# Half-sized weight requests for the sixth and seventh expert, moved ahead of a small table's store, and a vector's load moved behind them

## The chip, the cores and the metric

One core of one Trainium2 chip runs the whole kernel. The metric is the device time of one execution in microseconds (us), from a median of three runs. The core has a matrix engine (TensorE, PE in the rows), a vector engine (DVE), a scalar engine (ACT), GpSimd (POOL), and SyncE (SP), which here only asks for transfers. Sixteen DMA engines carry the transfers that SP's queue (q1 in the profile) and POOL's queue (q0) ask for.

## What is computed

One decoder layer over 1024 prompt tokens and 64 sample tokens, 1024 wide: a mixer (S5 and RG-LRU), cross attention, a mixture of experts, and a final norm. The change lies in the mixture of experts:

```python
def _hier_moe(x, g, w_group, w_expert, w_gate, w_up, w_down):
    hf = _rmsnorm(x, g).reshape(bsz * s, D_MODEL)
    ...                                    # top 1 of 4 groups, then top 2 of its 8 experts
    act = jax.nn.silu(jnp.einsum("td,edf->tef", hf, w_gate)) * jnp.einsum("td,edf->tef", hf, w_up)
    out = jnp.einsum("tef,efd->td", act * combine[..., None].astype(act.dtype), w_down)
    return out.reshape(bsz, s, D_MODEL).astype(x.dtype)
```

There are 32 experts; each has a gate and an up matrix of 1024 x 256 floats (1 MB each) and a down matrix of 256 x 1024 floats (1 MB). The kernel's output is the norm of x + out, times the vector `g_final`.

## The kernel before

The engines' programs are written out by hand, each engine in its own function, with semaphores between them; nothing reorders them. In the last stage the tokens are sorted by expert into slots: each expert has 96 slots, and 24 rounds of 128 slots go through all 32 experts, four thirds of an expert per round (`expert_of`). Rounds 0 and 1 use experts 0, 1 and 2. A round j is, on TensorE: `rows_t` (L1292, the gathered rows of a later round turned), `prod_t` (L1311), `gate_up(j + 1)` (L1304, 64 matmuls over k = 0 to 7) and `down(j)` (L1318, 32 matmuls). `gate_up(1)` is cut in two, k = 0 to 3 and k = 4 to 7, with the turn of round 2's rows between.

Weights go through rings of buffers in the on-chip memory: five slots for gate and up together (`gu`, GUB = 5) and five for down (`dn`). Experts 0 to 4 are loaded before the rounds begin. Expert e + 5 takes the slot of expert e, so its load waits until the last round that uses e has been through `gate_up` (semaphore `gu_full`, one per round) or `down` (`d_full`). `last_round(e)` says which round that is: 1 for experts 0 and 1, then 2 for experts 2 and 3, and so on. All these loads are issued by SP, in program order, `load_gu` as two transfers of 1 MB (L487), `load_dn` as one (L490).

POOL gathers the rows of each round by an indirect transfer (`fetch`, L640) from a table in memory, `work_rows`, whose row is the token's 1024 values and a tail of four values (its routing weights). Rounds 0 to 3 are gathered before the tails are there, and get theirs by small gathers of their own (L650). The tails are then stored by SP (`weights_out(xrows[:, D:RW], "wt_st")`, two transfers, L439 and L440: 1088 rows of 16 bytes). SP waits for the gathers of rounds 0 to 3 before that store (L531), since it writes the table that they read. POOL's gather of round 4 waits for `wt_st` (L704), and round 4's rows are turned by TensorE between `down(1)` and `gate_up(3)`. On POOL the store of round 0's result (L645) and the gather of round 5 come next.

`gfin` is `g_final` copied to all 128 partitions (L533, 512 KB); it is first used by the vector engine when the first finished rows are scaled (L2708).

Around the change SP's program is: the down weights of expert 4; the wait for the gathers of rounds 0 to 3; the tails' store; `gfin`; then, for each round, the loads that its end lets go.

Of the kernel before, what the change touches and what calls it, by code (L numbers as in the profile page):

```python
# [7 lines left out]
D = 1024  # L8
P = 128
# [17 lines left out]
NG, NE, FF = 4, 32, 256  # L27
# [3 lines left out]
GUB, DNB, XGB = 5, 5, 5  # L31
# [27 lines left out]
ys5_ok w_sum wout_in q_full q_free q_sum wo_in0 wo_in1 x_res0 x_res1 x_res2 sq2_ok xn2_ok xn2_st0  # L59
xn2_st1 mx_ok pn_ok smx_ok spn_ok ck_in0 ck_in1 ck_in2 cv_in0 cv_in1 cv_in2 consts_ok route_ok gexp_ok  # L60
a_ok r48_ok ctl_ok idx_ok gu_in0 gu_in1 gu_in2 gu_in3 gu_in4 dn_in0 dn_in1 dn_in2 dn_in3 dn_in4
xg_in0 xg_in1 xg_in2 xg_in3 t_full t_free gu_full silu_ok prod_ok rk_full ix_full dve_x ht_full htm_ok
d_full ya_ok zt_ok y_st0 y_st1 x_go xw_in role_ok wt_ok wt_st yg_in0 yg_in1 yg_in2 yg_in3
o_st0 o_st1 o_st2 o_st3 z_ok ss_ok pw_arg pw_ok std2_ok o_ok own_ok xg_in4 y_st2
yg_in4 o_st4 gath_in"""
# [2 lines left out]
def hybrid_layer(nc, I, O, W):  # L68
# [5 lines left out]
    with ctx:  # L74
# [3 lines left out]
        sem = {n: ctx.enter_context(nc.semaphore(n)) for n in SEMS.split()}  # L78
# [238 lines left out]
        gu = [reg(a, 2, KD, FF) for a in (0, 4096, 8192, R_UT, R_UT + 4096)]  # L317
        dn = [reg(a, 2, D) for a in [R_E2 + 2048 * s for s in range(4)] + [R_R]]
        RW = D + WT
# [5 lines left out]
        gfin = reg(R_Y + D * YGB, D)  # L325
# [5 lines left out]
        xrows = nc.dram_tensor("work_rows", (TOK, RW), f32, kind="Internal").ap()  # L331
# [16 lines left out]
        def expert_of(j, t):  # L348

            return ((0, 0, 1, 1), (0, 1, 2, 2))[j][t] if j < 2 else (4 * j + t) // 3  # L350

        def last_round(e):

            return max(1, (3 * e + 2) // 4)
# [5 lines left out]
        def _(sp):  # L360
# [77 lines left out]
            def weights_out(table, done):  # L438
                sp.dma_start(table[0:SEQ, :].rearrange("(i p) c -> p i c", p=P), wt[:, 0:NT - 1, :]).then_inc(sem[done], 16)  # L439
                sp.dma_start(table[SEQ:TOK, :], wt[0:ROWS[NT - 1], NT - 1, :]).then_inc(sem[done], 16)  # L440
# [44 lines left out]
            def load_gu(e, slot, s):  # L485
                for h, w in enumerate(("w_gate", "w_up")):
                    sp.dma_start(gu[slot][:, h, :, :], weights(w, e, "p k")).then_inc(s, 16)  # L487

            def load_dn(e, slot, s):
                sp.dma_start(dn[slot][:, :, :], weights("w_down", e, "k p")).then_inc(s, 16)  # L490

# [35 lines left out]
            weights_out(wtab, "lam_in")  # L527
            sp.wait_ge(sem["xg_in1"], 16)
            load_dn(4, 4, sem["dn_in4"])
            for c in range(4):  # L530
                sp.wait_ge(sem[f"xg_in{c}"], 16)  # L531
            weights_out(xrows[:, D:RW], "wt_st")
            sp.dma_start(gfin[:, :], I["g_final"].to_broadcast([P, D])).then_inc(sem["glu_in"], 16)  # L533
            for j in range(NR + 1):
                for e in range(NE - GUB):
                    if last_round(e) == j:
                        sp.wait_ge(sem["gu_full"], j + 1)
                        load_gu(e + GUB, e % GUB, sem[f"gu_in{e % GUB}"])
                for e in range(NE - DNB):
                    if last_round(e) == j - 1:  # L540
                        sp.wait_ge(sem["d_full"], j)
                        load_dn(e + DNB, e % DNB, sem[f"dn_in{e % DNB}"])
# [226 lines left out]
        def _(pe):  # L769
# [99 lines left out]
            for j in range(7):  # L869
                last = nc.tensor.transpose(b[:, j * GP:j * GP + GP], q16[0:GP, 11 + j, :], ident[0:GP, 0:GP])  # L870
            last.then_inc(sem["tp_full"], 1)
            pe.wait_ge(sem["bnat_in"], 16 * 18)
            for ri in range(2):
                b = claim(TP, tp, "tp_free")
                for j in range(4):
                    last = nc.tensor.transpose(b[:, j * P:j * P + P], craw[:, ri, j, :], ident[:, :])
# [3 lines left out]
            for ri in range(2):  # L880
                last = nc.tensor.transpose(b[:, ri * P:ri * P + P], stin[ri], ident[:, :])
# [7 lines left out]
            for q in range(4):  # L889
                for ri in range(2):  # L890
                    for j in range(4):
                        gp = q * 4 + j
                        for l in range(2):
                            last = nc.tensor.matmul(bl[l][32 * j:32 * j + GC, q * P:q * P + P], bbar[64 * l:64 * l + 64, ri, gp, :],
                                                    hmat[64 * l:64 * l + 64, ri, gp, 0:L, :].rearrange("p t c -> p (t c)"), start=ri == 0, stop=ri == 1)
# [5 lines left out]
            for gp in range(GP):  # L901
                b = claim(TAY, ta, "ta_free")
                for ri in range(2):
                    for l in range(2):
                        last = nc.tensor.matmul(b[64 * l:64 * l + 64, ri * CS:ri * CS + CS], gmat[:, gp, ri, 64 * l:64 * l + 64],
                                                uch[:, 2 * gp + l, :], start=True, stop=True)
# [52 lines left out]
            for t0, t1 in TSPLIT:  # L959
                for m in range(CT):  # L960
                    b = claim(MA, ma, "ma_free")
                    for k in range(CT):
                        last = nc.tensor.matmul(b[:, 0:(t1 - t0) * CS], wglu[:, k, m * P:m * P + P], yd[:, k, t0 * CS:t1 * CS], start=k == 0, stop=k == CT - 1)  # L963
# [9 lines left out]
            for ri in range(2):  # L973
                last = nc.tensor.transpose(b[0:GP, (2 + ri) * P:(3 + ri) * P], finp[:, ri, :], ident[:, :])
# [322 lines left out]

            def gate_up(j, k0=0, k1=KD):
                for e in experts(j):
                    pe.wait_ge(sem[f"gu_in{e % GUB}"], (e // GUB + 1) * 32)  # L1300
                for k in range(k0, k1):
                    for t in range(4):
                        e, t0 = expert_of(j, t), QT * t
                        last = nc.tensor.matmul(bank[2 + j % 2][t0:t0 + QT, :].rearrange("p (h n) -> p h n", h=2), (xgt[j % 2] if j else xgt_first)[:, k, t0:t0 + QT],  # L1304
                                                gu[e % GUB][:, :, k, :], start=k == 0, stop=k == KD - 1)
                if k1 == KD:
                    last.then_inc(sem["gu_full"], 1)

# [128 lines left out]
            for j in range(1, NR):  # L1437
# [12 lines left out]
                if j == NR - 2:  # L1450
# [6 lines left out]
                    for nh in range(2):  # L1457
                        last = residual(j, nh, False)
# [12 lines left out]
            with pe.If(pe.value_load(ctl[0:1, XT:XT + 1], min_val=0, max_val=XT) > 0):  # L1471
                pe.wait_ge(sem["o_ok"], NR)
                for c in (NR - 2, NR - 1):
                    for nh in range(2):
                        last = down_half(c, nh)
# [1379 lines left out]
```

## Time and profile before

| | |
|---|---|
| times of three runs | 1103.89, 1108.48, 1109.3 us; median 1108.48 |
| profiled execution, its own time | 1104.57 us, span 1102.8 us |
| TensorE busy | 1064.1 us, 96% of the span |
| VectorE, ScalarE, GpSimd busy | 63%, 26%, 17% |
| DMA | 204.97 MB, mean 186 GB/s over the span; 412 to 415 GB/s in most of the slices from 860 to 1050 us |

The span is what lies between the first and the last instruction of the profiled execution; 1.8 us lie around it. "DMA share" in the rows is the mean busy share of the 16 DMA engines in a stretch (1.00 is all of them, a little above is rounding at the edges), and GB/s what they moved. A share near 1 with few GB/s means that the engines hold packets that move slowly. Times in rows are from the span's start. In a row of the chain "DMA arena<-in_w_up" with its microseconds is the time from the request of a load to its landing.

### The profile page before, as it was taken

What the parts mean: (1) busy time and instruction counts of PE and PEld (TensorE: products, weight loads), DVE (VectorE), ACT (ScalarE), POOL (GpSimd) and SP (SyncE); (2) the same over time, 40 slices, a digit from 0 to 9 for tenths busy, and PEclk for the clock granted to TensorE, in tenths of its full rate; (3) what the DMA queues carried; (4) which work ended last, traced back from release to release, by engine and by line L of the source; (5) the groups of instructions that cost most, each with busy time, mean ns of one, the idle gap of its engine ahead of it and who ended that gap; (6) DMA issues with size and microseconds to landing.
All of it is one profiled execution on the core that took longest, in us unless ns stands there. A gap on an engine that the chain in (4) does not pass through costs nothing.

```text
span 1102.8 us, 15605 instructions
## 1 busy us (share of the span) xinstructions
PE 1064.1 (96%) x6135; PEld 607.6 (55%) x6135; DVE 695.9 (63%) x1385; ACT 289.4 (26%) x588; POOL 186.2 (17%) x229
## 2 busy tenths in 40 slices
PE   6999999999999999999999999989999999998996
PEld 4666766787764445888766645545533333333331
DVE  5576699947858665743376676877754455555453
ACT  5200341567821111100033301111411222222223
POOL 4000200101000000000000000000123445554455
PEclk9999999999999999999999999999999999999999
DMA  9109450297546004100244450015889999999962
GB/s 297 56 1 213 46 43 1 92 276 257 216 170 182 1 1 155 74 1 1 85 183 154 155 226 39 20 58 208 299 283 412 413 413 413 414 415 412 413 256 82
DMA packets 75468, 204.97 MB, mean 186 GB/s; under 512 B 25592, under 2 KB 34448, under 8 KB 67056
## 3 DMA queue, kind: packets, MB, share of 16 engines
q1 hardware_dynamic: 54336, 168.82, 43.4%
q0 software_dynamic: 20928, 35.09, 9.6%
q8 instruction: 50, 0.82, 0.3%
q14 instruction: 26, 0.21, 0.1%
q10 hardware_dynamic: 128, 0.03, 0.0%
HBM read 195.23 MB, written 52.18 MB: 224 GB/s over the span
## 4 chain that ended last, share of the span: by engine, by line
PE 77%; DMA 10%; DVE 5%; ACT 2%; SPq 2%; issue 2%; ACTq 0%; POOL 0%; POOLq 0%; DVEq 0%
PE bank L832 16%; PE bank L1004 9%; PE bank L1069 9%; PE bank L1304 8%; DMA arena<-in_w_up 7%; PE bank L1199 6%; PE bank L1318 4%; PE bank L802 3%; PE bank L963 3%; PE bank L1101 3%; PE bank L1166 3%; DMA arena<-in_w_down 2%; DMA arena<-work_rows,slots_in 1%; SPq L487 1%; PE bank L1248 1%
## 5 line engine op out<-in xcount | busy, mean ns | idle before, releaser
L832 PE MATMUL bank<-arena 128*128 128x360 f32 (+1 forms) x576 | 177.7, 468 | 0.9 <-DVE arena L1881 0.9
L1304 PE MATMUL bank<-arena 128*32 128x512 f32 x1536 | 172.3, 599 | 5.9 <-DMA arena<-in_w_up 5.9
L832 PEld LDWEIGHTS bank<-arena 128*128 128x128 f32 x576 | 108.5, 190 | 64.7 <-issue 1.4
L1304 PEld LDWEIGHTS bank<-arena 128*32 128x32 f32 x1536 | 50.4, 110 | 107.5 <-issue 107.1
L2200 DVE TENSOR_TENSOR arena<-arena,bank 128x512 f32<-128x512 f32 (+3 forms) x56 | 68.4, 1221 | 64.9 <-PE bank L1069 37.4
L1004 PE MATMUL bank<-arena 128*128 128x272 f32 x448 | 103.0, 392 | 0.0
L1199 PE MATMUL bank<-arena 128*128 128x512 f32 x224 | 100.6, 598 | 2.2 <-DVE arena L2365 2.2
L1069 PE MATMUL bank<-arena 128*128 128x512 f32 x224 | 97.7, 593 | 0.0
L1004 PEld LDWEIGHTS bank<-arena 128*128 128x128 f32 x448 | 85.0, 190 | 17.4
L1318 PE MATMUL bank<-arena 128*32 128x512 f32 x768 | 87.5, 593 | 1.3 <-DMA arena<-in_w_down 0.8
L2696 DVE SCALAR_TENSOR_TENSOR arena<-arena 128x1024 f32<-128x1024 f32 x22 | 45.8, 2083 | 66.5 <-ACT arena L1763 66.5
L1523 ACT ACTIVATE arena<-bank 128x272 f32<-128x272 f32 (+5 forms) x94 | 41.8, 450 | 170.4 <-PE bank L832 122.1
L1069 PEld LDWEIGHTS bank<-arena 128*128 128x128 f32 x224 | 41.9, 190 | 50.6 <-issue 50.6
L1199 PEld LDWEIGHTS bank<-arena 128*128 128x128 f32 x224 | 41.0, 190 | 47.6 <-issue 47.5
L1673 ACT ACTIVATE arena<-arena 128x1024 f32<-128x1024 f32 (+1 forms) x18 | 19.0, 1057 | 170.4 <-DVE arena L2200 151.5
L802 PE MATMUL bank<-arena 128*128 128x256 f32 x256 | 57.7, 382 | 0.3 <-ACT arena L1523 0.2
L1318 PEld LDWEIGHTS bank<-arena 128*32 128x32 f32 x768 | 26.3, 110 | 56.4 <-issue 55.7
L802 PEld LDWEIGHTS bank<-arena 128*128 128x128 f32 x256 | 47.8, 190 | 10.5 <-issue 4.4
L640 POOL DMA_INDIRECT arena<-work_rows,slots_in x24 | 27.9, 1162 | 149.9 <-DVE slots_in L2577 117.8
L2705 DVE TENSOR_TENSOR arena<-arena 128x1024 f32<-128x1024 f32 x22 | 26.9, 1224 | 39.2 <-DMA arena<-work_firsts,ptmp 39.2
L2288 DVE TENSOR_TENSOR arena<-bank,arena 128x272 f32<-128x272 f32 x48 | 20.4, 440 | 47.5 <-PE bank L1004 47.4
L1881 DVE TENSOR_TENSOR arena<-bank,par 128x512 f32<-128x512 f32 (+1 forms) x58 | 35.8, 657 | 21.1 <-PE bank L788 19.9
(474 smaller groups left out, 1457.3 us busy)
## 6 DMA issues: line engine op xcount, KB each, us to landing
arena<-in_w_gate SPq DMA_DIRECT2D x32, 1024.0 KB, 18.9
arena<-in_w_up SPq DMA_DIRECT2D x32, 1024.0 KB, 25.1
arena<-in_w_down SPq DMA_DIRECT2D x32, 1024.0 KB, 26.4
arena<-in_ck SPq DMA_DIRECT2D x8, 1024.0 KB, 7.1
arena<-in_cv SPq DMA_DIRECT2D x8, 1024.0 KB, 5.4
arena<-in_w_in SPq DMA_DIRECT2D x3, 2048.0 KB, 13.7
work_firsts<-in_x SPq DMA_DIRECT2D x1, 4352.0 KB
arena<-in_x SPq DMA_DIRECT2D x8, 512.0 KB, 5.9
```

The lines of the kernel that those rows point to most:

```text
L802: last = nc.tensor.matmul(b[:, 0:KQ], mt_[:, k, m * P:m * P + P], wkv[q % 3][:, k, :], start=k == 0, stop=k == KD - 1)
L832: last = nc.tensor.matmul(b[:, 0:w], win[slot][:, k, m * P:m * P + P], ht[:, k, c0:c0 + w], start=k == 0, stop=k == KD - 1)
L963: last = nc.tensor.matmul(b[:, 0:(t1 - t0) * CS], wglu[:, k, m * P:m * P + P], yd[:, k, t0 * CS:t1 * CS], start=k == 0, stop=k == CT - 1)
L1004: last = nc.tensor.matmul(b[:, 0:QN], a_(k, m), b_(k)[:, QN * n:QN * n + QN], start=k == 0, stop=k == 3)
L1069: last = nc.tensor.matmul(b[:, :], a_(k), b_(k), start=k == 0, stop=k == 3)
L1199: last = nc.tensor.matmul(b[:, :], a_(k), b_(k), start=k == 0, stop=k == 3)
L1304: last = nc.tensor.matmul(bank[2 + j % 2][t0:t0 + QT, :].rearrange("p (h n) -> p h n", h=2), (xgt[j % 2] if j else xgt_first)[:, k, t0:t0 ...
L1318: last = nc.tensor.matmul(bank[DB[j] + nh][t0:t0 + QT, :], htr[j % 2][:, k, t0:t0 + QT], dn[e % DNB][:, k, nh * 512:nh * 512 + 512], start ...
L1523: nc.scalar.activation(out, bank[ring[n % len(ring)]][0:out.shape[0], 0:w] if isinstance(w, int) else w(bank[ring[n % len(ring)]]), func, ...
L1881: V.tensor_tensor(out_cols(hf), b[:, :].rearrange("p (k t) -> p k t", k=4)[:, :, 0:r], cols[:, 4 * hf:4 * hf + 4].unsqueeze(2).to_broadcas ...
L2200: V.tensor_tensor(out, out, bank[banks(n)][:, :].unsqueeze(1).to_broadcast([P, width, 512]), ADD).then_inc(sem["md_free"], 1)
L2696: V.scalar_tensor_tensor(split(y), by_column(xg[b]), m1[:, slot:slot + 1], split(y), MUL, ADD).then_inc(sem["zt_ok"], 1)
```

## The change

The gate and up weights of experts 5 and 6 (the sixth and seventh; they take the slots of experts 0 and 1, whose last round is round 1) are each loaded as two halves of k, so eight transfers of 512 KB instead of four of 1 MB. The halves for k = 0 to 3 wait for a new semaphore, `gu_half`, which TensorE raises at k = 3 of every `gate_up`; those for k = 4 to 7 wait for `gu_full` as before. The first halves stand ahead of the wait for the gathers and the tails' store, the second halves behind it; `gfin` comes after them. The counts that `gate_up` waits for follow (`gate_fills`). The sizes of all other loads, and the order of all others, stay.

```diff
+        def in_halves(e):
+            return e >= GUB and last_round(e - GUB) == 1
+        def gate_fills(e):
+            return sum(64 if in_halves(o) else 32 for o in range(e % GUB, e + 1, GUB))
...
+            def load_gu_half(e, slot, k0):
+                for h, w in enumerate(("w_gate", "w_up")):
+                    sp.dma_start(gu[slot][:, h, k0:k0 + 4, :], weights(w, e, "p k")[:, k0:k0 + 4, :]).then_inc(sem[f"gu_in{slot}"], 16)
...
-            for c in range(4):
-                sp.wait_ge(sem[f"xg_in{c}"], 16)
-            weights_out(xrows[:, D:RW], "wt_st")
-            sp.dma_start(gfin[:, :], I["g_final"].to_broadcast([P, D])).then_inc(sem["glu_in"], 16)
             for j in range(NR + 1):
+                for k0 in (0, 4):
+                    for e in range(NE - GUB):
+                        if last_round(e) == j and in_halves(e + GUB):
+                            sp.wait_ge(sem["gu_full" if k0 else "gu_half"], j + 1)
+                            load_gu_half(e + GUB, e % GUB, k0)
+                    if (j, k0) == (1, 0):
+                        for c in range(4):
+                            sp.wait_ge(sem[f"xg_in{c}"], 16)
+                        weights_out(xrows[:, D:RW], "wt_st")
                 for e in range(NE - GUB):
-                    if last_round(e) == j:
+                    if last_round(e) == j and not in_halves(e + GUB):
                         sp.wait_ge(sem["gu_full"], j + 1)
                         load_gu(e + GUB, e % GUB, sem[f"gu_in{e % GUB}"])
+                if j == 1:
+                    sp.dma_start(gfin[:, :], I["g_final"].to_broadcast([P, D])).then_inc(sem["glu_in"], 16)
...
                 for e in experts(j):
-                    pe.wait_ge(sem[f"gu_in{e % GUB}"], (e // GUB + 1) * 32)
+                    pe.wait_ge(sem[f"gu_in{e % GUB}"], gate_fills(e))
...
+                    if k == 3:
+                        last.then_inc(sem["gu_half"], 1)
```

SP's program before, from the down weights of expert 4 (first row) to the down weights that the end of round 1 lets go (last row). `arena` is the on-chip memory, `work_rows<-wt` the tails, and a bracket names the semaphores that a request waits for:

```order
L490 DMA arena<-in_w_down 128x2x1024 [waits xg_in1]
L439 DMA work_rows<-wt 128x8x4 [waits xg_in2,xg_in3,xg_in1,xg_in0]
L440 DMA work_rows<-wt 64x4
L533 DMA arena<-in_g_final 128x1024
L487 DMA arena<-in_w_gate 128x2048 [waits gu_full]
L487 DMA arena<-in_w_up 128x2048
...
L490 DMA arena<-in_w_down 128x2x1024 [waits d_full] x2
```

The same place now, first as far as the tails' store (line numbers are those of the changed kernel):

```order
L502 DMA arena<-in_w_down 128x2x1024 [waits xg_in1]
L499 DMA arena<-in_w_gate 128x1024 [waits gu_half]
L499 DMA arena<-in_w_up 128x1024
L499 DMA arena<-in_w_gate 128x1024 [waits gu_half]
L499 DMA arena<-in_w_up 128x1024
L447 DMA work_rows<-wt 128x8x4 [waits xg_in2,xg_in3,xg_in1,xg_in0]
L448 DMA work_rows<-wt 64x4
```

and on from there to the first loads that round 2 lets go:

```order
L499 DMA arena<-in_w_gate 128x1024 [waits gu_full]
L499 DMA arena<-in_w_up 128x1024
L499 DMA arena<-in_w_gate 128x1024 [waits gu_full]
L499 DMA arena<-in_w_up 128x1024
L557 DMA arena<-in_g_final 128x1024
L495 DMA arena<-in_w_gate 128x2048 [waits gu_full]
```

Four requests have come ahead of the tails, and the vector has gone from in front of experts 5 and 6 to behind them; it still stands ahead of round 2's loads.

POOL's program keeps its order. Its place that depends on the tails, as it stands now (L669 the small gathers, L659 a gather of rows, L664 the store of a round's result):

```order
L669 DMA arena<-work_wtab,slots_in 128x4 [waits xg_in3]
L659 DMA arena<-work_rows,slots_in 128x1028 [waits wt_st]
L664 DMA work_firsts<-arena,slots_in 1088x1024 [waits zt_ok,small_out,idx_ok]
L659 DMA arena<-work_rows,slots_in 128x1028 [waits zt_ok]
L664 DMA work_firsts<-arena,slots_in 1088x1024 [waits zt_ok]
```

Nothing moved there; the gather of round 4 still waits for the tails, and the store of round 0's result and the gather of round 5 still stand behind it.

## Rows read from the trace of the kernel before

**Rows 1.** Page: the span, busy times, and the DMA lines of forty slices.

```profile
span 1102.8 us, 15605 instructions
PE 1064.1 (96%) x6135; PEld 607.6 (55%) x6135; DVE 695.9 (63%) x1385; ACT 289.4 (26%) x588; POOL 186.2 (17%) x229
GB/s 297 56 1 213 46 43 1 92 276 257 216 170 182 1 1 155 74 1 1 85 183 154 155 226 39 20 58 208 299 283 412 413 413 413 414 415 412 413 256 82
```

**Rows 2.** Windows of the last stage: stretch, length, busy engines, clock, DMA share, GB/s.

```profile
800.00:805.00 5.00, 5.00 (x49) 1.70 (x51) 4.51 (x20) 0.00 (x0) 0.19 (x1) 1.00 0.85 137
805.00:808.00 3.00, 3.00 (x28) 1.27 (x24) 2.76 (x12) 0.00 (x0) 2.39 (x3) 1.00 0.69 274
808.00:810.00 2.00, 2.00 (x24) 0.52 (x16) 0.64 (x2) 0.00 (x0) 1.42 (x2) 1.00 0.38 14
810.00:814.00 4.00, 4.00 (x38) 1.86 (x38) 0.42 (x1) 0.38 (x1) 0.99 (x1) 1.00 0.99 170
814.00:820.00 6.00, 6.00 (x64) 1.82 (x56) 3.90 (x7) 1.92 (x4) 0.44 (x1) 1.00 1.02 422
820.00:928.00 108.00, 107.24 (x978) 37.30 (x966) 54.77 (x82) 26.21 (x52) 49.96 (x55) 1.00 1.02 413
928.00:1057.00 129.00, 121.01 (x1078) 46.49 (x1078) 65.77 (x91) 32.42 (x63) 66.00 (x71) 0.99 1.02 410
1057.00:1092.80 35.80, 35.72 (x244) 10.77 (x236) 18.48 (x30) 12.47 (x28) 22.84 (x22) 1.00 0.42 145
```

**Rows 3.** The chain that ended last, from 986 us: start, length, what.

```profile
986.69 3.79 SPq L487
990.48 0.04 issue
990.52 27.64 DMA arena<-in_w_up
1018.16 0.14 issue
1018.30 8.80 PE bank L1304 x64
1027.10 0.02 issue
1027.12 3.65 SPq L487
1030.76 0.04 issue
1030.81 25.86 DMA arena<-in_w_up
1056.67 0.14 issue
```

**Rows 4.** SP's requests in order of time: start, length, line, transfer.

```profile
798.74 0.38 SPq L490 DMA_DIRECT2D arena<-in_w_down  x1
807.22 0.37 SPq L439 DMA_DIRECT2D work_rows<-wt  x1
807.63 0.59 SPq L440 DMA_DIRECT2D work_rows<-wt  x1
808.26 0.59 SPq L533 DMA_DIRECT2D arena<-in_g_final  x1
810.42 0.34 SPq L487 DMA_DIRECT2D arena<-in_w_gate  x1
811.83 0.51 SPq L487 DMA_DIRECT2D arena<-in_w_up  x1
818.82 0.33 SPq L487 DMA_DIRECT2D arena<-in_w_gate  x1
```

**Rows 5.** TensorE in order of time: `gate_up(1)`'s first piece and two turns of rows.

```profile
802.15 3.62 PE L1304 MATMUL bank<-arena 128*32 128x512 f32 x32
805.69 1.09 PE L1292 MATMUL bank<-ident,arena 128*128 128x128 f32 x8
822.12 1.09 PE L1292 MATMUL bank<-ident,arena 128*128 128x128 f32 x8
```

**Rows 6.** Windows of one us, columns as in the second group.

```profile
807.00:808.00 1.00, 1.00 (x12) 0.26 (x8) 0.93 (x5) 0.00 (x0) 0.70 (x2) 1.00 0.27 96
808.00:809.00 1.00, 1.00 (x16) 0.37 (x12) 0.64 (x2) 0.00 (x0) 0.70 (x2) 1.00 0.57 26
809.00:810.00 1.00, 1.00 (x16) 0.15 (x7) 0.00 (x0) 0.00 (x0) 0.72 (x1) 1.00 0.19 1
```

**Rows 7.** Transfers issued from 650 to 850 us: size, median us to landing.

```profile
work_rows<-arena SPq DMA_DIRECT2D x8, 512.0 KB, 3.2
arena<-in_g_final SPq DMA_DIRECT2D x1, 512.0 KB, 6.2
work_rows<-wt SPq DMA_DIRECT2D x1, 16.0 KB, 3.0
work_rows<-wt SPq DMA_DIRECT2D x1, 1.0 KB, 3.2
```

**Rows 8.** Windows early in the span, where 512 KB loads of x stream.

```profile
4.00:6.00 2.00, 0.00 (x0) 0.00 (x0) 0.00 (x0) 1.64 (x3) 0.00 (x0) 1.00 1.04 407
10.00:12.00 2.00, 0.56 (x4) 0.25 (x2) 1.93 (x7) 0.00 (x0) 0.00 (x0) 1.00 1.03 387
```

**Rows 9.** POOL in order of time: the gather of round 4, and what follows.

```profile
811.61 0.99 POOL L640 DMA_INDIRECT arena<-work_rows,slots_in  x1 [1.89 <-DMA work_rows<-wt]
819.56 1.02 POOL L645 DMA_INDIRECT work_firsts<-arena,slots_in  x1 [6.96 <-DVE arena L2696]
```

**Rows 10.** Gathers of rows, 760 to 850 us, to landing; then the chain's longest.

```profile
DMA to landing us min/median/max: 4.2/9.5/11.3
...
911.86 16.44 DMA arena<-work_rows,slots_in
```

**Rows 11.** TensorE at the round that begins at 1015 us.

```profile
1018.30 8.77 PE L1304 MATMUL bank<-arena 128*32 128x512 f32 x64 [1.97 <-DMA arena<-in_w_up]
1031.67 7.07 PE L1304 MATMUL bank<-arena 128*32 128x512 f32 x64
```

More of the change, by code:

```diff
@@ L61 @@
 a_ok r48_ok ctl_ok idx_ok gu_in0 gu_in1 gu_in2 gu_in3 gu_in4 dn_in0 dn_in1 dn_in2 dn_in3 dn_in4
-xg_in0 xg_in1 xg_in2 xg_in3 t_full t_free gu_full silu_ok prod_ok rk_full ix_full dve_x ht_full htm_ok
+xg_in0 xg_in1 xg_in2 xg_in3 t_full t_free gu_half gu_full silu_ok prod_ok rk_full ix_full dve_x ht_full htm_ok
 d_full ya_ok zt_ok y_st0 y_st1 x_go xw_in role_ok wt_ok wt_st yg_in0 yg_in1 yg_in2 yg_in3
```

## The prediction

> **What bounds the kernel now.** I read the page first. TensorE is busy for 96% of the span and the DMA engines move 412 to 415 GB/s in most of the late slices [rows 1], so the page alone would name TensorE. The windows of the last stage name another. From 820 to 928 us TensorE is idle for 108.00 - 107.24 = 0.76 us; from 928 to 1057 us for 129.00 - 121.01 = 7.99 us; after that hardly at all. The DMA engines are full (share 1.02, 410 to 422 GB/s) from 814 to 1057 us without a pause, and mostly idle after [rows 2]. So up to some 928 us the weights loaded ahead cover a deficit, and from there TensorE waits for transfers, 8.75 us in all. The chain says the same in order of time: a request for up weights waits 27.64 us to land, TensorE works, the next waits 25.86 us, and the last of these lands at 1056.67 us [rows 3]. A load that takes 26 us for 1 MB is one in a long queue. Behind 1057 us TensorE has its work without a gap.
>
> The reader should take one rule from this: the end stands where the DMA engines have finished a fixed amount of bytes, plus what TensorE does after it. Transfer work that is done earlier anywhere between 805 and 1057 us moves the end by as much, up to the 8.75 us that TensorE waits. A wait on TensorE in between costs nothing as long as it is shorter than the waits that it replaces, and while the DMA queue stays filled.
>
> **What the first halves gain.** The stretch that the change works on is 805 to 814 us. From 808 to 810 the DMA engines have a share of 0.38 and move 14 GB/s; from 810 to 814 they are full and move 170 GB/s [rows 2]. Before, SP stands at its wait until 807.22, stores the tails, asks for the vector at 808.26, and for experts 5 and 6 from 810.42 to 812.34, when `gate_up(1)` is through [rows 4]. Now it can ask for the first halves when k = 3 of `gate_up(1)` is done, which is when the first of its two pieces ends and the turn of rows begins, near 805.7 [rows 5]. Four requests at about 0.45 us each [rows 4] take until 807.6. The vector was asked for at 808.26 and the engines fill up at 810, so a request needs some 1.7 us before its packets move; the first halves then move from 807.5.
>
> The idle time that they fill is: half of 807 to 808 at share 0.27 (0.37 us), 808 to 809 at 0.57 (0.43 us), 809 to 810 at 0.19 (0.81 us) [rows 6]: 1.6 us. Four halves are 2.1 MB, 5.0 us at 418 GB/s, so they last until the second halves are there; these are asked for from about 810.4 on, at the same time as the whole loads before. No gap opens between.
>
> What the halves cost beside whole loads: their runs are half as long. The nearest row is that of 512 KB loads of x, which stream at 387 to 407 GB/s against 413 [rows 2, 8]. Of 4.2 MB (10.2 us) that is 1.5 to 6%, 0.15 to 0.65 us; I take 0.2, from the stretch where the share is 1.04, since in the other the queue also held small transfers.
>
> A rule of the Trainium skill speaks against this part: "DMA: Bandwidth & Descriptors", section Bandwidth, wants transfers of 1 MiB or more, and its section on the anatomy of a DMA gives each a fixed part of about 2 us, so that by it (an estimate from that page) four further requests would cost 8 us if nothing overlapped. The 387 to 407 GB/s of the 512 KB loads here [rows 8] speak against it for loads that stand in one queue.
>
> **The vector.** Its 512 KB took 6.2 us to land, where a store of the same size took 3.2 [rows 7], and the 4 us from 810 to 814, in which it moves, run at 170 instead of 418 GB/s [rows 2]: (1 - 170 / 418) x 4 = 2.4 us lost. All 128 partitions read the same 4 KB of memory; that this is what is slow I only infer. Behind the halves it is asked for at about 812.4 instead of 808.26 and moves at some 818 to 821. If it is as slow there, nothing is gained or lost; if, with the 16 engines no longer all at it at once, it holds up only some of them, up to 2.4 us come back. Bounds 0 and 2.4; I take 0.6, near the lower end, since the nearest row is its own. Its first use is after the first finished rows come back, beyond 850 us, so its later landing costs nothing.
>
> **The tails and the gather behind them.** The tails are asked for at about 807.65 instead of 807.22, but behind 2.1 MB in the same queue. Before, they landed 3.0 and 3.2 us after request [rows 7], 810.2 and 810.8, and POOL issued round 4's gather at 811.61 after 1.89 us of waiting for them [rows 9]. Now they land about 4 to 5 us later, and the gather goes out near 816. Gathers land after 4.2 to 11.3 us there, median 9.5 [rows 10]. From 811.61 the median gives 821.1, a little ahead of the turn of round 4's rows at 822.12 [rows 5], where TensorE had no wait. From 816 it gives 825.5: a wait of about 3.4 us on TensorE where there was none, between nothing (820.2) and 5.2 us (827.3). I take 3.4. What is queued behind the gather on POOL is the store of round 0's result, which waited 6.96 us for the vector engine and went out at 819.56 [rows 9]; it has room for the delay.
>
> Of the ring order the Trainium skill says the same ("DMA: Bandwidth & Descriptors", Queues, rings and completion order: each engine takes a ring's descriptors in order); by that the tails cannot overtake the halves. If they could, the 3.4 us would be 0 to 0.4, and the end the same.
>
> These 3.4 us are not on the path to the end: they come out of the 8.75 us that TensorE waits later. The queue keeps filled meanwhile, since whatever round 1 and 2 let go, two experts' halves, two whole experts and two down matrices, is asked for before or at 822 us and is 10 MB, 25 us of work.
>
> **Small edits, at nothing.** The increments at k = 3 (24 of them) ride on matmuls, and the first piece of `gate_up(1)` is followed by the turn of rows without a gap [rows 5]; bounds 0 and, were each to cost the 0.04 us that the chain shows as an issue [rows 3], 1 us of TensorE, which the later waits would take in. Four more requests on SP take 1.9 us there, before a wait of 6 us for round 2's end (812.34 to 818.82 [rows 4]).
>
> **The sum.** 1.6 (idle filled) - 0.2 (shorter runs) + 0.6 (vector) = 2.0 us earlier, with bounds 1.6 - 0.65 = 0.95 and 1.6 - 0.15 + 2.4 = 3.9. Against the profiled execution's own time: 1104.57 - 2.0 = 1102.6. The runs shown lie in two pairs, 1103.89 and 1104.57, 1108.48 and 1109.3, and nothing in the profile says which pair the next median will be near; from the median it is 1106.5. I forecast the middle, 1104.5, and mean by it a gain of 2 us on a base of 1106.5.
>
> **Rivals.** *Nothing gained*: the four halves only change places with the tails and the vector. That would be so if requests take longer than 1.7 us to move while POOL's gathers are at work (share 0.85 at only 137 GB/s from 800 to 805 [rows 2]). Time 1106.5. *All of it gained*: the whole stretch 805.8 to 814 runs at 418 GB/s. Of 808 to 810 that is 1.9 us, of 810 to 814 2.4, of 807 to 808 0.7: 5.0 us, 1101.5. For it: full engines with few bytes are waiting on something that other work could fill. Against: the vector and 1088 tails of 16 bytes still have to go through the same engines. *The gather takes the waits' place, and more*: under a full queue a gather took 16.44 us in the chain [rows 10]. From 816 that ends at 832.4, a wait of 10.3 us on TensorE at round 2. It decides once the wait is longer than the 8.75 us that it replaces: 10.3 - 8.75 = 1.6 us later. A wait may cost more: at 1018.30, behind 1.97 us of idling, `gate_up` took 8.77 instead of 7.07 us [rows 11]; with one such, 3.3 us: 1109.8. Against it: no gather before 850 us took over 11.3. *Each half pays for itself*: 512 KB takes 3.2 us to land alone [rows 7] and 1.25 at 418 GB/s; if the 1.95 between were paid for each of four further requests, 7.8 us less the 2.0 gained: 1112.3. This is the rule on transfers under 1 MiB, weighed above; the 407 GB/s speak against it.
>
> **How the numbers follow.** Forecast (a gain of about 1 to 4 us) 0.60; nothing gained 0.17; all gained 0.14; the gather 0.06; each half 0.03. The range: the lower pair less 4 us is about 1100; the upper pair with nothing gained is about 1109.3. From 1100.0 to 1109.3 it holds all but the worst of the last two and some of the all-gained case. Faster by over 0.5% (about what a measurement of this kernel can tell from no change) means under 1102.9 against 1108.48: a fifth of the forecast's cases, where the median falls into the lower pair, and half of the all-gained case, 0.12 + 0.07 = 0.19, and I say 0.20. Slower by over 0.5% is over 1114: 0.03 for the last rival and 0.01 for the gather. Same 0.76.
>
> **What would show it.** Right: four 512 KB requests from 805.7 to 807.6; DMA share near 1 and over 350 GB/s from 808 to 810; POOL's gather of round 4 at 815 to 817; a wait of 1 to 5 us on TensorE ahead of the turn at 822; less waiting from 928 to 1057 us, by about that plus 2 us; the last up weights for `gate_up(22)` 1 to 4 us earlier than 1056.67. Wrong: the last weights land no earlier, or TensorE is without waits after 928 us and still ends later; or the waits after 928 vanish altogether, which would mean that the transfers were not the limit.

## The result and the profile after

| | before | changed |
|---|---|---|
| median of 20 runs each | 1107.16 us (1103.42 to 1109.3) | 1110.57 us (1107.02 to 1113.94) |
| changed to before | | 1.0038, 95% interval 1.0026 to 1.005 |
| profiled execution, span | 1104.57, 1102.8 us | 1112.26, 1110.5 us |

The changed kernel is slower: the medians differ by 3.4 us, and the ratio of 1.0038 stands for 4.2 us (2.9 to 5.5). That is within the 0.5% which the forecast called the same, but on the other side of its 2 us gain, and outside its range, which ended at 1109.3.

The two profiled spans differ by 7.7 us, more than the medians. The first piece of `gate_up(1)` begins at 802.15 us before [rows 5] and at 807.40 in the changed kernel, 5.25 us later, ahead of all that the change touches. In windows from 700 to 800 us (columns as in [rows 2]) the granted clock of the profiled execution before is 1.00, that of the changed kernel 0.97:

```profile
700.00:800.00 100.00, 95.31 (x488) 53.39 (x488) 71.46 (x255) 18.97 (x40) 5.19 (x6) 1.00 0.46 161
```
```profile
700.00:800.00 100.00, 95.79 (x456) 52.33 (x454) 71.00 (x249) 18.46 (x39) 2.33 (x3) 0.97 0.43 154
```

Profiled executions of kernels below that leave this part alone fall on either side of that as well, so I measure the change from the beginning of `gate_up(1)` to the end of the last `down`: 802.15 to 1092.72, 290.57 us before, and 807.40 to 1100.42, 293.02 us in the changed kernel. The change costs 2.45 us there; it is this "stage" that the experiments give.

First the requests of SP in the changed kernel, then the landing of the tails and the vector (transfers issued from 809 to 830 us), then POOL's gather of round 4 and what follows:

```profile
811.08 0.34 SPq L499 DMA_DIRECT2D arena<-in_w_gate  x1
813.10 0.54 SPq L447 DMA_DIRECT2D work_rows<-wt  x1
813.68 1.83 SPq L448 DMA_DIRECT2D work_rows<-wt  x1
815.67 1.01 SPq L499 DMA_DIRECT2D arena<-in_w_gate  x1
818.44 0.45 SPq L557 DMA_DIRECT2D arena<-in_g_final  x1
```
```profile
arena<-in_g_final SPq DMA_DIRECT2D x1, 512.0 KB, 11.8
...
work_rows<-wt SPq DMA_DIRECT2D x1, 16.0 KB, 7.6
work_rows<-wt SPq DMA_DIRECT2D x1, 1.0 KB, 8.3
```
```profile
822.71 0.99 POOL L659 DMA_INDIRECT arena<-work_rows,slots_in  x1 [7.74 <-DMA work_rows<-wt]
826.41 1.02 POOL L664 DMA_INDIRECT work_firsts<-arena,slots_in  x1 [2.70 <-DVE arena L2717]
```

The tails are asked for 5.70 us behind the beginning of `gate_up(1)`, where it was 5.07 before [rows 4, 5], and land after 7.6 and 8.3 us instead of 3.0 and 3.2 [rows 7]. POOL waits 7.74 us for them instead of 1.89 [rows 9], and the gather goes out 15.3 us behind that beginning instead of 9.5. That is 5.85 us later. TensorE, at the place where it had no wait before [rows 5]:

```profile
823.83 3.62 PE L1339 MATMUL bank<-arena 128*32 128x512 f32 x32
831.93 1.97 PE L1311 MATMUL bank<-ident,arena 128*128 128x128 f32 x8 [4.48 <-DMA arena<-work_rows,slots_in]
833.70 0.63 PE L1332 MATMUL bank<-ident,arena 128*128 128x128 f32 x2
834.26 8.26 PE L1323 MATMUL bank<-arena 128*32 128x512 f32 x64
842.35 3.61 PE L1339 MATMUL bank<-arena 128*32 128x512 f32 x32
```

It waits 4.48 us for round 4's rows, and what follows takes 1.97, 0.63 and 8.26 us where the same work a round later takes 1.09, 0.38 and 7.07: 2.3 us more. Windows say why: the clock. TensorE idles from 827.45 us on, and from 829.9 to 836.8 us it is granted at 0.51 on the mean, the lower of its two levels:

```profile
813.25:815.25 2.00, 2.00 (x24) 0.52 (x16) 0.64 (x2) 0.00 (x0) 1.43 (x2) 1.00 0.97 328
815.25:819.25 4.00, 4.00 (x38) 1.87 (x38) 0.42 (x1) 0.38 (x1) 0.00 (x0) 1.00 1.01 291
819.25:825.25 6.00, 6.00 (x64) 1.81 (x56) 2.30 (x4) 1.92 (x4) 0.99 (x1) 1.00 1.09 306
825.25:833.25 8.00, 3.52 (x30) 1.71 (x20) 4.18 (x9) 1.26 (x2) 3.07 (x3) 0.79 1.02 389
...
829.90:836.80 6.90, 4.87 (x26) 2.62 (x30) 2.26 (x3) 0.38 (x1) 1.90 (x2) 0.51 1.02 422
```

So round 2 ends 6.8 us late. The first three of these windows answer to 808 to 820 us of [rows 2]: 328, 291 and 306 GB/s in 2, 4 and 6 us, 3.66 MB, against 14, 170 and 422, 3.24 MB before. The idle time is filled, and 0.42 MB more is through at the end of it, 1.0 us of work. Little of this lasts: the vector, which had landed by 814.5 us before [rows 4, 7], lands here only at 830.2, and the next 8 us move 389 GB/s, where the kernel before moved this:

```profile
820.00:828.00 8.00, 8.00 (x78) 2.92 (x70) 3.83 (x7) 1.59 (x3) 2.63 (x3) 1.00 1.02 425
```

That is 0.29 MB less. With the vector through, the lead is 0.13 MB, 0.3 us.

From there on TensorE's waits are of another kind. Those of the kernel before, 928 to 1060 us, and then those of the changed kernel from 806 to 1101 us (engine, line and what it waited for: us, times, longest):

```profile
PE bank L1304 <- DMA arena<-in_w_up: 5.9, 6, 2.0
PE bank L1292 <- DMA arena<-work_rows,slots_in: 1.9, 2, 1.0
```
```profile
PE bank L1311 <- DMA arena<-work_rows,slots_in: 8.3, 4, 4.5
PE bank L1357 <- DMA arena<-work_firsts,ptmp: 1.2, 1, 1.2
```

Not one wait for weights is left. In their place stand, beside the 4.48 us, 3.8 us for gathered rows (1.9 before) and 1.2 for rows of first results. The chain that ended last goes through POOL there, no more through requests for weights [rows 3]:

```profile
990.57 15.56 DMA work_firsts<-arena,slots_in
...
1008.26 1.00 POOL arena L659
...
1018.86 18.05 DMA arena<-work_rows,slots_in
...
1036.96 1.09 PE bank L1311 x8
```

A store of a round's result takes 15.56 us to land; POOL, which waits for it before it fetches from that table, issues gathers behind that wait, and a gather takes 18.05 us.

### The profile page after: what moved, and what is told of

Its sections match the earlier page's. It is cut to its first block, busy times and chain, and to the rows that moved or that the text cites. A ratio compares the mean times of both kernels' runs of the same rounds, so it can differ in the third digit from the quotient of the medians.

```text
span 1110.5 us, 15609 instructions
## 1 busy us (share of the span) xinstructions
PE 1071.0 (96%) x6135; PEld 605.5 (55%) x6135; DVE 696.5 (63%) x1385; ACT 288.9 (26%) x588; POOL 189.8 (17%) x229
## 4 chain that ended last, share of the span: by engine, by line
PE 77%; DMA 9%; DVE 5%; issue 3%; ACT 3%; POOL 2%; ACTq 0%; SPq 0%; POOLq 0%; DVEq 0%
PE bank L851 16%; PE bank L1023 9%; PE bank L1088 9%; PE bank L1323 7%; PE bank L1218 7%; DMA work_firsts<-arena,slots_in 5%; PE bank L1339 4%; PE bank L821 3%; PE bank L982 3%; PE bank L1120 3%; PE bank L1185 2%; DMA arena<-work_rows,slots_in 2%; DMA arena<-work_firsts,ptmp 2%; PE bank L1005 1%; PE bank L1267 1%
## 5 line engine op out<-in xcount | busy, mean ns | idle before, releaser
L1323 PEld LDWEIGHTS bank<-arena 128*32 128x32 f32 x1536 | 47.3, 111 | 105.5 <-issue 105.1
L1694 ACT ACTIVATE arena<-arena 128x1024 f32<-128x1024 f32 (+1 forms) x18 | 19.0, 1057 | 172.0 <-DVE arena L2221 151.5
L1339 PEld LDWEIGHTS bank<-arena 128*32 128x32 f32 x768 | 24.4, 110 | 57.0 <-issue 55.7
L659 POOL DMA_INDIRECT arena<-work_rows,slots_in x24 | 25.2, 1052 | 157.9 <-DVE slots_in L2598 119.5
```

What stands on the lines that cost most here:

```text
L1339: last = nc.tensor.matmul(bank[DB[j] + nh][t0:t0 + QT, :], htr[j % 2][:, k, t0:t0 + QT], dn[e % DNB][:, k, nh * 512:nh * 512 + 512], start ...
```

## The experiments

Ratios are to the kernel before, measured beside it, with 95% intervals. The stage and the delay come from one profile of each kernel. The delay at round 2 is what TensorE lost between `down(1)` and the end of `gate_up(3)`.

| kernel | ratio | stage, us | delay at round 2, us |
|---|---|---|---|
| before | 1 | 290.57 | 0 |
| changed | 1.0038 (1.0026 to 1.0050) | 293.02 | 6.8 |
| tails first | 1.0005 (0.9993 to 1.0018) | 289.99 | 0 |
| halves of k, not early | 1.0009 (0.9996 to 1.0022) | 291.07 | 0 |
| halves of partitions, not early | 1.0113 (1.0099 to 1.0128) | 302.06 | (two waits) |
| tails behind whole loads | 1.0053 (1.0040 to 1.0066) | 294.94 | 10.0 |
| vector late alone | 1.0021 (1.0009 to 1.0033) | 291.85 | 0 |
| changed, wait filled, 32 | 1.0031 (1.0014 to 1.0048) | 294.88 | 7.2 |
| before, 36 fillers | 1.0039 (1.0024 to 1.0054) | 292.90 | 8.1 |
| round 4 with a small gather | 1.0047 (1.0031 to 1.0063) | 289.40 | 0 |
| before, 18 fillers | 1.0011 (0.9997 to 1.0026) | 290.36 | 4.1 |
| changed, wait filled, 18 | 1.0011 (0.9998 to 1.0025) | 291.35 | 5.4 |
| vector early alone | 0.9997 (0.9983 to 1.0010) | 290.12 | 0 |
| tails first, halves and vector early | 0.9996 (0.9981 to 1.0010) | 287.93 | 0 |

My first two theories were: S, the halves themselves are slow transfers; G, the late gather of round 4 is the loss.

**Tails first.** The changed kernel, with the tails' store ahead of the first halves:

```diff
+            for c in range(4):
+                sp.wait_ge(sem[f"xg_in{c}"], 16)
+            weights_out(xrows[:, D:RW], "wt_st")
             for j in range(NR + 1):
...
-                    if (j, k0) == (1, 0):
-                        for c in range(4):
-                            sp.wait_ge(sem[f"xg_in{c}"], 16)
-                        weights_out(xrows[:, D:RW], "wt_st")
```

> The changed kernel with one thing undone: the tails are stored before the first halves are asked for; halves, early request and late vector stay. Theory S (the halves are slow transfers: in the profile of the changed kernel they move at about 280 GB/s with the DMA engines full, so 4.2 MB of them cost some 4.9 us more than whole loads, and this work sets the end): slower than the kernel before by 2 to 4 us, and halves at 250 to 330 GB/s. Theory G (the tails behind the halves make the gather of round 4 late, TensorE waits 4.5 us at round 2 and then runs 2.3 us longer at the lower clock): no wait at round 2, and 0 to 2 us faster than before.

No loss is left that can be told from nothing: 1.0005. POOL's gather of round 4 goes out 8.4 us behind the beginning of `gate_up(1)` (801.92 here), and TensorE's waits from 800 to 1093 us are of the kind of the kernel before again:

```profile
810.35 1.00 POOL L658 DMA_INDIRECT arena<-work_rows,slots_in  x1 [0.84 <-DMA work_rows<-wt]
```
```profile
PE bank L1322 <- DMA arena<-in_w_up: 7.1, 7, 2.0
PE bank L1310 <- DMA arena<-work_rows,slots_in: 1.5, 2, 0.9
PE bank L1338 <- DMA arena<-in_w_down: 0.8, 2, 0.5
```

Only the order of four requests and two differs from the changed kernel, and with it the loss goes. S falls here as the cause: the halves are still there.

**Halves of k, not early.** The kernel before, with `load_gu` of experts 5 and 6 as eight halves at its old place:

```diff
...
-                        load_gu(e + GUB, e % GUB, sem[f"gu_in{e % GUB}"])
+                        if e < 2:
+                            load_gu_half(e + GUB, e % GUB, 0)
+                            load_gu_half(e + GUB, e % GUB, 1)
+                        else:
+                            load_gu(e + GUB, e % GUB, sem[f"gu_in{e % GUB}"])
...
```

> The kernel before, with the loads of experts 5 and 6 cut into halves of k (4 KB runs, one in every 8 KB), all asked for where the whole loads were; nothing is early, the tails and the vector keep their places. Theory S: slower than before by 3 to 5 us, the halves at 250 to 330 GB/s. Theory G: within 1 us of before, since the tails are as early as they were. Forecast's own size for the halves (387 to 407 GB/s): 0.2 to 0.7 us slower.

1.0009, about 1.0 us, not told apart from nothing. The halves are asked for from 812.55 us on. While the first of them move, the engines are nearly full at 287 GB/s, a rate that S named; while the others do, they move 420:

```profile
814.00:820.00 6.00, 6.00 (x60) 1.82 (x56) 1.30 (x4) 1.54 (x3) 0.46 (x1) 1.00 0.96 287
820.00:830.00 10.00, 10.00 (x98) 3.57 (x90) 6.41 (x10) 1.98 (x4) 3.06 (x3) 1.00 1.03 420
```

**Halves of partitions, not early.** The same, cut by 64 partitions:

```diff
...
+                    sp.dma_start(gu[slot][64 * k0:64 * k0 + 64, h, :, :], weights(w, e, "p k")[64 * k0:64 * k0 + 64, :, :]).then_inc(sem[f"gu_in{slot}"], 16)
...
```

> As the run with halves of k, but each load is cut by partitions: 64 partitions a request, runs of 8 KB as in a whole load; the number and the size of requests are those of the halves of k. Theory S with the gaps in memory as the cause: within 1 us of before, at 400 GB/s and more. Theory S with the size or number of requests as the cause: slower by 3 to 5 us as well. Theory G: within 1 us of before.

All theories missed: 12.5 us slower. With full DMA engines these transfers move at half the rate for some 20 us:

```profile
820.00:830.00 10.00, 6.12 (x57) 1.80 (x50) 5.55 (x8) 1.65 (x3) 2.06 (x2) 0.96 1.02 203
830.00:840.00 10.00, 10.00 (x82) 4.00 (x85) 1.47 (x3) 0.77 (x2) 3.03 (x3) 0.87 1.04 238
```

It tells nothing of the change, only that the way a load is cut can cost far more than its place.

**Tails behind whole loads.** No halves; the tails behind expert 5's whole load, the vector last:

```diff
-            weights_out(xrows[:, D:RW], "wt_st")
-            sp.dma_start(gfin[:, :], I["g_final"].to_broadcast([P, D])).then_inc(sem["glu_in"], 16)
...
                         load_gu(e + GUB, e % GUB, sem[f"gu_in{e % GUB}"])
+                        if e == 0:
+                            weights_out(xrows[:, D:RW], "wt_st")
+                if j == 1:
+                    sp.dma_start(gfin[:, :], I["g_final"].to_broadcast([P, D])).then_inc(sem["glu_in"], 16)
```

> Whole loads of 1 MB as before, but the tails are stored behind the load of expert 5, and the vector comes behind expert 6: the tails' delay without any halves. POOL's gather of round 4 should go out near 819 instead of 811.6 us, and TensorE should wait 4 to 8 us at round 2. Theory G: slower than before by 3 to 6 us. Theory S: within 1.5 us of before, since the wait at round 2 is taken out of the waits that come later.

5.9 us slower, without any halves. The vector is late here as well, which alone costs 2.3 us (next run); some 3.5 us are left for the late tails. TensorE at round 2:

```profile
835.09 1.97 PE L1294 MATMUL bank<-ident,arena 128*128 128x128 f32 x8 [7.51 <-DMA arena<-work_rows,slots_in]
...
837.41 8.39 PE L1306 MATMUL bank<-arena 128*32 128x512 f32 x64
```

So G holds as to where. G does not say why waits of 4.48 and 7.51 us were not made up by the 8.75 us of later waits, as the forecast had it. The next ones ask that.

**Vector late alone.** The kernel before with the vector behind experts 5 and 6 and nothing else moved:

```diff
-            sp.dma_start(gfin[:, :], I["g_final"].to_broadcast([P, D])).then_inc(sem["glu_in"], 16)
...
+                if j == 1:
+                    sp.dma_start(gfin[:, :], I["g_final"].to_broadcast([P, D])).then_inc(sem["glu_in"], 16)
```

> The kernel before with the vector alone moved behind the loads of experts 5 and 6; whole loads, tails as early as before. The forecast's term for the vector: 0.6 us faster, between 0 and 2.4. If transfers are not what sets the end by themselves: within 1 us of before.

2.3 us slower, with the wrong sign for the forecast's 0.6 us. The windows that answer to 808 to 820 us before (`gate_up(1)` begins at 807.35 here):

```profile
813.20:815.20 2.00, 2.00 (x24) 0.52 (x16) 0.63 (x2) 0.00 (x0) 1.42 (x2) 1.00 0.04 1
815.20:819.20 4.00, 4.00 (x38) 1.86 (x38) 1.73 (x5) 1.93 (x4) 1.00 (x1) 1.00 0.62 203
819.20:825.20 6.00, 6.00 (x64) 1.82 (x56) 3.06 (x7) 0.39 (x1) 2.05 (x2) 1.00 1.01 396
```

Where the vector was slow before (170 GB/s at share 0.99) the engines now stand idle for a third of the time, since the whole loads cannot be asked for earlier. In the 12 us 3.19 MB are through, against 3.24 before, and the vector, which those 3.24 contain, is still to come. I read this so: the vector was slow in time that was otherwise lost, and is now work in the full stretch. No rows add up to the 2.3 us (1.0 to 3.7).

**Before, with fillers.** In the kernel before, small matmuls without use ahead of the turn of round 4's rows: a delay of TensorE with no transfer moved and no idling.

```diff
+                if j == 2:
+                    pe.wait_ge(sem["t_free"], 2 * j + 4)
+                    for _ in range(36):
+                        nc.tensor.matmul(bank[0][:, 0:P], ident[:, :], ident[:, :], start=True, stop=True)
                 if j + 2 < NR:
```

> The kernel before with 36 such matmuls (4.4 us) at the same place: TensorE is 4.4 us late at round 2, but no transfer is moved and the clock is not touched. The forecast's rule (the end stands where a fixed amount of bytes is through, a delay on TensorE comes out of later waits): within 1 us of before. Theory P (a delay of the rounds also delays all transfers that hang on rounds, the gathers, stores and outputs, while the weights run ahead, so the delay comes back as waits for gathers): 2 to 4.4 us slower than before.

> The kernel before with 18 filling matmuls at round 2. In the run with 36 they took 8.1 us, not 4.4, so these take 4.1 us; this is the size that was meant. If a delay comes out of the later waits as long as it is smaller than they are (8.54 us of waits there, and 5.4 to 6 of another kind that stay whatever the delay): 0 to 1.5 us slower than before. If each us of delay costs half a us or more: 2 us or more slower.

Each filler is two matmuls in the trace (72 for 36), so 36 took 8.1 us, not the 4.4 that I meant, and 18 took 4.1 (first kernel, then second):

```profile
824.12 8.30 PE L1441 MATMUL bank<-ident 128*128 128x128 f32 x72
832.26 1.04 PE L1292 MATMUL bank<-ident,arena 128*128 128x128 f32 x8
```
```profile
824.42 4.29 PE L1441 MATMUL bank<-ident 128*128 128x128 f32 x36
828.55 1.04 PE L1292 MATMUL bank<-ident,arena 128*128 128x128 f32 x8
```

A delay of 4.1 us is made up as far as can be told (the stage is 0.2 us shorter than before; the ratio is 1.0011 with 1 in its interval, which reaches to 2.9 us). One of 8.1 us is not: 1.0039, 4.3 us (2.3 in the stage), though it is smaller than the 8.75 us of waits. And already with 4.1 us the waits have changed kind (803 to 1096 us):

```profile
PE bank L1292 <- DMA arena<-work_rows,slots_in: 4.9, 6, 1.4
...
PE bank L1304 <- DMA arena<-in_w_up: 0.5, 1, 0.5
```

**Changed, wait filled.** The changed kernel with 32 and with 18 of these matmuls in its wait:

```diff
+                if j == 2:
+                    pe.wait_ge(sem["t_free"], 2 * j + 4)
+                    for _ in range(32):
+                        nc.tensor.matmul(bank[0][:, 0:P], ident[:, :], ident[:, :], start=True, stop=True)
```

> The changed kernel with 32 small matmuls (3.9 us) whose results nobody uses put where TensorE waits for round 4's rows, so that it does not idle there. The rows come as late as in the changed kernel, so the end can move only by what follows from idling: if the lower clock behind the wait costs, the clock stays at 1.00 through round 2, the 2.3 us go, and the kernel is 0.5 to 2.5 us faster than the changed one (1 to 3 us slower than before). If the clock costs nothing in the end, the same as the changed kernel, 3 to 4 us slower than before.

> The changed kernel with 18 filling matmuls (4.1 us) in the wait of round 2, which was 4.48 us long; with 32 they took longer than the wait. If the lower clock behind the wait is a part of the loss: the clock stays at 1.00 behind the wait, and the kernel is 1 to 2.5 us faster than the changed one, 1 to 2.5 us slower than before. If not: as the changed kernel, 3 to 4 us slower than before.

With 32 they took 7.2 us, longer than the wait; the clock stayed up at round 2, but the delay was 7.2 us, and the loss stayed (1.0031). With 18 they fit:

```profile
825.67 4.29 PE L1462 MATMUL bank<-ident 128*128 128x128 f32 x36
831.04 1.09 PE L1311 MATMUL bank<-ident,arena 128*128 128x128 f32 x8 [1.08 <-DMA arena<-work_rows,slots_in]
...
832.28 7.07 PE L1323 MATMUL bank<-arena 128*32 128x512 f32 x64
```

The rows come late as in the changed kernel, but `gate_up(3)` takes 7.07 us instead of 8.26, and the ratio is 1.0011 (0.9998 to 1.0025), below the whole interval of the changed kernel. Useless work on an idle engine takes back 3 us by the ratios, 1.7 in the stage: the lower clock behind the wait is a part of the loss. The delay falls only from 6.8 to 5.4 us, since the rows land 1.08 us behind the fillers here.

**Round 4 with a small gather.** The changed kernel, with round 4 gathered early, as rounds 0 to 3, without its tails; the tails' store then waits for five gathers:

```diff
...
+            fetch(4, 4, "xg_in4")
             pool.wait_ge(sem["lam_in"], 128)
-            for c in range(4):
+            for c in range(5):
                 pool.wait_ge(sem[f"xg_in{c}"], 16)
-                weights_of(c, c, "gath_in")
+                weights_of(c, c, "gath_in" if c < 4 else "own4_in")
             pool.wait_ge(sem["wt_st"], 32)
-            fetch(4, 4, "xg_in4")
...
```

> The changed kernel, but round 4 is gathered without its tails, right behind rounds 0 to 3, and gets them by a small gather of its own as these do, so it waits for no tails; the tails are stored behind the gather of round 4. Theory G (all of the loss comes from the late gather of round 4): no wait at round 2, and 0 to 2 us faster than before, as the run with the tails first or better. If something else in the change costs: still 2 us or more slower than before.

The stage says G: no wait at round 2, and 289.40 us, 1.2 less than before. The time says the opposite, 1.0047. The difference lies behind the last work. The last instruction that the trace lists is POOL's output, here and then in the kernel before:

```profile
1099.03 0.98 POOL L681 DMA_INDIRECT out_y_s<-arena,ptmp  x1 [0.30 <-issue]
```
```profile
1097.58 0.98 POOL L662 DMA_INDIRECT out_y_s<-arena,ptmp  x1 [0.30 <-issue]
```

It ends at 1100.0 in a span of 1109.5 us; before, the same one ends at 1098.6 of 1102.8. So some 5 us more pass at the end, in a kernel with one indirect transfer more on POOL and one semaphore more (the changed kernel, with one semaphore more than before, has no such end). What passes there I did not find out. By the expectation's own terms G missed; since the excess lies outside the stage, I count this run neither for G nor against it.

**Vector early.** The vector behind the down weights of expert 3, once in the kernel before, once with tails first and early halves:

```diff
             load_dn(3, 3, sem["dn_in3"])
+            sp.dma_start(gfin[:, :], I["g_final"].to_broadcast([P, D])).then_inc(sem["glu_in"], 16)
...
-            sp.dma_start(gfin[:, :], I["g_final"].to_broadcast([P, D])).then_inc(sem["glu_in"], 16)
```

> The kernel before with the vector asked for some 23 us earlier, behind the down weights of expert 3 (785 us), so that its slow 4 us are off the stretch from 810 on. If the weights' landing sets the end: 1 to 3 us faster than before. If the gathers of rounds 1 to 3 are held up by it and the tails with them: 1 to 4 us slower, with a wait at round 2.

> The tails first, the first halves early as in the change, and the vector behind the down weights of expert 3: what is left of the change when each of its losses is undone. If the weights' landing sets the end: 1 to 4 us faster than before, and faster than the kernel with the tails first and the vector late (1.0005 of before). If the vector there holds up the gathers: slower than that one.

0.9997 and 0.9996: not told apart from the kernel before, although the stage of the second was 2.6 us shorter in its one profile. The stage leaves out what the vector does ahead of it: in the second, TensorE waited 0.96 us for gathered rows just before the stage began at 806.62:

```profile
803.85 1.09 PE L1309 MATMUL bank<-ident,arena 128*128 128x128 f32 x8 [0.96 <-DMA arena<-work_rows,slots_in]
```

No version here beats the kernel before by more than can be measured.

## Why the prediction was wrong

**Bound, half right.** That the DMA engines are full from 814 to 1057 us and that TensorE waits for weights at the end of it is so in the kernel before. The rule drawn from it, that a wait in between costs nothing up to the 8.75 us that it replaces, is the step that failed. Fillers of 4.1 us cost nothing that could be told, 8.1 us of them cost 4.3 us. The room, a delay less what it cost, is 3.8 us there by the ratio and 5.8 by the stage, and from 2.6 (the changed kernel, by the ratio) to 5.6 (tails behind whole loads, by the stage) in the others that cost something: not 8.75. Of the later waits only those for weights (5.9 and 0.76 us) give way; 1.9 us were for gathered rows from the start, and waits for rows now come to 3.8 to 4.9 us, whichever kind of delay it was. That the waits after 928 us vanish was named in the forecast as a sign of being wrong; those for weights did. A part of the room was no wait either: the kernel before loses 1.7 us at 1018.30 to the lower clock [rows 11], and with 18 or 36 fillers no `gate_up` takes over 7.08 us. I read the rest as follows; the traces show the pieces, no run isolates it. Weights are asked for by SP as soon as slots are free; stores, gathers and outputs hang on the rounds, in POOL's queue, behind landings of 15 us and more. A late TensorE lets weights run ahead and pushes the rows' transfers back, so the bytes that I took as fixed ahead of the end are not the same bytes.

**The gather, right in place and nearly in size.** Predicted: issued 4 to 5 us later, 9.5 us to land, a wait of 3.4 us (0 to 5.2). Measured: 5.85 us later, 9.2 us to land, 4.48 us. SP's second request for the tails took 1.83 us where 0.59 stood before [rows 4]. The tails landed behind the halves. The forecast cited the Trainium skill for this ("DMA: Bandwidth & Descriptors", Queues, rings and completion order: each engine takes a ring's descriptors in order); the landing of the tails, 7.6 and 8.3 us instead of 3.0 and 3.2, agrees with it. That they cannot overtake is more than that section of the Trainium skill says, since it lets a later descriptor finish its write first.

**The clock, seen and put in the wrong place.** The forecast had a price for it, 1.7 us behind a wait of 1.97 us [rows 11], but only in the rival with the slow gather. The sum should have had it: behind 4.48 us it cost 2.3. The delay at round 2 was thus 6.8 us and not 3.4; 4.1 us could be made up, and 6.8 were not.

**That rival.** "The gather takes the waits' place, and more" was the right mechanism, with chance 0.06 and 1109.8 us. Its point of decision, a wait longer than 8.75 us, was the same mistake as above. That its time came near the measured 1110.57 us is luck: it took a wait of 10.3 us, and 4.48 were measured.

**First halves.** Predicted 1.6 us of idle time filled, less 0.2. The windows give 1.0 us of work ahead at 825.25 us, and 0.3 us once the late vector is through too, of the 2.0 us that the sum had; with the tails first this is too small to show in the time. The halves' own cost, 0.2 predicted, is 1.0 us with an interval from -0.4 to 2.4. The estimate of 8 us for four requests more, which the forecast worked out from the fixed part of about 2 us in the Trainium skill ("DMA: Bandwidth & Descriptors", section on the anatomy of a DMA; the page fits it on transfers that GpSimd issues, and these are SP's), is not borne out for loads in a full queue: it lies outside that interval. The rule of 1 MiB in the Trainium skill ("DMA: Bandwidth & Descriptors", section Bandwidth) is left open: halves of 512 KB moved at 287 GB/s for 6 us and then at 420.

**The vector.** Predicted 0.6 us gained, between 0 and 2.4; alone it costs 2.3 us. The lower bound of 0 was wrong for the move by itself. As I read it, a transfer that is slow while nothing else can be asked for costs nothing there, and costs its time wherever else it goes, unless the gap is filled by others, as with the tails first (1.0005, with the vector late).

**What stays open.** The stage explains 2.45 us. The medians differ by 3.4 and the ratio stands for 4.2 us, from 2.9 at the lower end of its interval; the rest was not found, and one profile of each is not enough to find it. How far the stage varies between executions of one kernel is not known either.

## What to carry to other kernels

Before a request is moved ahead of a small one in the same queue, follow who waits for the small one, through other engines, down to the engine that sets the end; here 17 KB of tails behind 2.1 MB of weights cost more than the weights gained. Waits further on are room for a delay only as far as what they wait for does not itself hang on the delayed work; fillers of two sizes on the waiting engine measure that room. And a wait on TensorE is priced with what it runs at afterwards.

## What the runs showed of the hardware

- Loads of 64 of the 128 partitions moved at 203 to 238 GB/s for 20 us with the DMA engines full, where halves of the same size and number that span 128 partitions moved at 287 GB/s for 6 us and then at 420. The kernel was 12.5 us slower for the first.
- In a wait of 4.48 us the clock fell to its lower level and stood there for 6.9 us, 4.9 of them behind the wait; filled with 18 useless matmuls, the wait had no such fall, and the kernel was faster for it (1.0011 against 1.0038).
- One indirect transfer more on POOL, with one semaphore more, came with some 5 us more behind the last work of the program; seen in one kernel, cause not known.
